# One front stage, loaded and ordered another way: scale columns first, shift columns last

## The reference, cut to what matters

```python
mod = (jax.nn.silu(c) @ p['w_ada'] + p['b_ada'])[:, None, :]
sh1, sc1, gt1, sh2, sc2, gt2 = jnp.split(mod, N_MOD, axis=-1)
hn = rms_norm(x, p['g_pre_mix']) * (1.0 + sc1) + sh1
proj = hn @ p['w_in']
```

## Time and profile before

| | |
|---|---|
| median of 3 runs | 1458.52 us (1458.16 to 1465.44) |
| profiled execution, its own time | 1462.23 us |
| its span | 1460.4 us |
| front stage, from the span's start to PE's last product in it | about 313 us |
| busy over the span | PE 87%, DVE 73%, ACT 52%, POOL 42% |

### The profile page before, as it was taken

One profiled execution on the slowest core, in us unless ns is written; L12 is line 12 of the kernel. 1 busy time (PEld: TensorE's weight loads), 2 busy tenths in 40 slices (PEclk: granted clock), 3 DMA queues, 4 the chain that ended last, 5 costly groups with the idle time before them and its releaser, 6 DMA issues. The chain is left out here.

```text
span 1460.4 us, 23246 instructions
## 1 busy us (share of the span) xinstructions
PE 1268.3 (87%) x6894; PEld 963.1 (66%) x6894; DVE 1069.1 (73%) x1980; ACT 753.6 (52%) x1609; POOL 616.1 (42%) x735
## 2 busy tenths in 40 slices
PE   5999999969898999699999998169999999999820
PEld 1688888855565656478888887048888888886300
DVE  3788878737786778557777764799999999993026
ACT  2432223213455758534444443148898899894134
POOL 1107767842232881012333221135665666564115
PEclk9999999987999989999999999579999999999975
DMA  9523444468987645324444453855989888879999
GB/s 328 154 83 127 160 159 173 151 217 315 310 283 208 183 159 162 129 100 144 144 144 146 166 163 131 310 189 144 279 250 273 242 221 260 247 184 301 374 294 356
DMA packets 111574, 305.35 MB, mean 209 GB/s; under 512 B 22884, under 2 KB 47589, under 8 KB 103758
## 3 DMA queue, kind: packets, MB, share of 16 engines
q1 hardware_dynamic: 85110, 230.90, 45.0%
q0 software_dynamic: 19360, 55.88, 16.3%
q10 hardware_dynamic: 7024, 17.60, 3.4%
HBM read 307.81 MB, written 97.21 MB: 277 GB/s over the span
## 5 line engine op out<-in xcount | busy, mean ns | idle before, releaser
L2943 DVE TENSOR_TENSOR ex_w_lo<-route_wgu,ex_w_hi 128x1024 fp32r<-128x1024 f32 x152 | 178.9, 1219 | 3.2 <-issue 2.4
L2671 POOL DMA_INDIRECT scratch_acc<-route_o,ex_to x43 | 83.6, 1944 | 186.6 <-DMA scratch_acc<-route_o,ex_to 108.5
L2712 ACT ACTIVATE ex_w_hi<-route_wgu 128x1024 fp32r (+1 forms) x152 | 152.8, 1065 | 6.0 <-issue 3.2
L147 PE MATMUL fr_ps_m<-fr_whi,fr_hl 128*128 128x512 f32 (+1 forms) x384 | 138.8, 362 | 1.0 <-DVE fr_wlo L657 0.5
L149 PE MATMUL fr_ps_m<-fr_whi,fr_hl 128*128 128x512 f32 (+1 forms) x384 | 136.1, 355 | 0.0
L148 PE MATMUL fr_ps_m<-fr_wlo,fr_hl 128*128 128x512 f32 (+1 forms) x384 | 136.0, 354 | 0.0
L2036 POOL TENSOR_SCALAR mx_st<-mx_st 128x1 f32<-128x1 f32 x68 | 38.7, 569 | 228.3 <-ACT mx_j L2084 128.1
L147 PE MATMUL ex_ps_h<-ex_w_hi,ex_xT 128*128 128x512 f32 x304 | 122.5, 403 | 0.2
L148 PE MATMUL ex_ps_h<-ex_w_lo,ex_xT 128*128 128x512 f32 x304 | 119.0, 391 | 0.0
L147 PE MATMUL mx_ps_m<-mw_area,mx_hT 128*128 128x512 f32 x272 | 108.9, 401 | 4.1 <-issue 2.1
L148 PE MATMUL mx_ps_m<-mw_area,mx_hT 128*128 128x512 f32 x272 | 107.3, 395 | 0.0
(11 more groups left out here) (549 smaller groups left out, 3482.1 us busy)
## 6 DMA issues: line engine op xcount, KB each, us to landing
route_wd<-in_w_exp_down_dram SPq DMA_DIRECT2D x47, 1024.0 KB, 12.9
route_wgu<-in_w_exp_gate_dram SPq DMA_DIRECT2D x46, 1024.0 KB, 10.8
route_wgu<-in_w_exp_up_dram SPq DMA_DIRECT2D x46, 1024.0 KB, 13.6
scratch_rec<-fr_w SPq DMA_DIRECT2D x16, 1048.0 KB, 4.1
s_rec<-scratch_rec SPq DMA_DIRECT2D x32, 524.0 KB, 5.9
scratch_proj<-fr_io SPq DMA_DIRECT2D x16, 640.0 KB, 3.0
scratch_acc<-in_zeros_dram SPq DMA_DIRECT2D x18, 512.0 KB, 5.6
fr_w<-in_w_ada_dram SPq DMA_DIRECT2D x8, 1024.0 KB, 9.1
```

Source lines behind the costliest of these rows:

```text
L147: nc.tensor.matmul(out, hi, w_hi, start=first, stop=False)
L2671: pool.indirect_dma_start(T["acc"], bass.IndirectOffsetOnAxis(to[:, t:t + 1], 0), o[:, t % 2, :], None, compute_op=ALU.add).then_inc(sem(" ...
L2712: A(w_hi[:, par, c * PW:(c + 1) * PW], wgu[:, bass.ds(slot * (KD * 2 * DE) + c * PW, PW)], ACT.Copy).then_inc(S["w_rounded"], 1)
L2943: vec.tensor_tensor(w_lo[:, par, c * PW:(c + 1) * PW], wgu[:, bass.ds(slot * (KD * 2 * DE) + c * PW, PW)], w_hi[:, par, c * PW:(c + 1) * P ...
```

## The change

The eight units of `w_ada` become eight scale units (512 KB each, loaded first) and eight shift units (512 KB each, loaded last, behind `w_in` and the parameters). `fold` becomes `fold_scale` and `fold_shift`. The transposes of the parameters move from between units 1 and 2 to behind the fourth product block of tile 0. `product(1)` moves ahead of the samples' products, which now stand between tiles 1 and 2; the shift units' matmuls, the shift rows and the samples' transposes stand inside tile 0's end and tile 1's product; the bias row is made in `product(2)` and not in `product(1)`. Tile 0's `add_bias` moves to t = 2 and stands behind `turns((4,))` and `turns((8,))`. New buffer `late` (3072 columns) holds two blocks of `w_in` first and then what `Bm`, `Bb`, `NB` and `kq` held; the samples' result goes to `samp` and no longer to `proj`, so `stored` counts one store less. The diff, cut to its core (SyncE, POOL, ACT, PE, DVE in this order):

```diff
+            def scale_unit(u):
+                sp.dma_start(scales[u], T["w_ada"][0, u * P:(u + 1) * P, D:2 * D]).then_inc(unit_in[u], 16)
+
+            def shift_unit(u):
+                if u >= 5:
+                    sp.wait_ge(mod_mm, KD + u - 2)
+                elif u >= 2:
+                    sp.wait_ge(mod_mm, KD)
+                sp.dma_start(shifts[u], T["w_ada"][0, u * P:(u + 1) * P, 0:D]).then_inc(unit_in[u], 16)
+
+            def rows_in(k):
+                if k >= 4:
+                    sp.wait_ge(mod_mm, 5)
+                sp.dma_start(raw[k], T["w_in"][0, k * P:(k + 1) * P, :]).then_inc(w_in[k], 16)
...
-            unit(0)
-            unit(1)
...
+            for u in range(6):
+                scale_unit(u)
+            sp.wait_ge(cT_done, 1)
+            sp.dma_start(x[:, 0, :], xp[:, 0, :]).then_inc(x_in[0], 16)
+            for u in range(6, KD):
+                scale_unit(u)
+            for k in range(4):
+                rows_in(k)
+            sp.dma_start(x[0:NS, 1, :], xs).then_inc(x_in[1], 16)
+            for k in range(4, KD):
+                rows_in(k)
...
-            for u in range(2, 4):
...
-            for k in range(KD):
...
+            for u in range(KD):
+                shift_unit(u)
             sp.wait_ge(s_out, SAMPLE_OUT)
-            sp.dma_start(pv[0:NS, NPT, :], proj[0:NS, 0, :]).then_inc(stored[0], 16)
+            sp.dma_start(pv[0:NS, NPT, :], samp[0:NS, :]).then_inc(small_out, 16)
...
-            pool.wait_ge(w_in[KD - 1], 16)
+            pool.wait_ge(s_mm, EARLY_MM)
...
-            pool.wait_ge(e_ready, 1)
+            pool.wait_ge(powers_ready, TURNS)
+            pool.wait_ge(s_out, BIAS_IN)
+            pool.wait_ge(small_out, 16)
...
                 act.wait_ge(rstd_ready, t + 2 if t else 1)
-                if t:
-                    act.wait_ge(stored[(t + 1) % 2], (t + 1) // 2 * 16)
+                if t >= 2:
+                    act.wait_ge(stored[(t + 1) % 2], t // 2 * 16)
...
             square(2)
+            root(2)
+            move(1)
             out(0)
-            move(1)
-            root(2)
+            turn_rates()
+            move_s()
+            out(1)
             square(3)
+            root(3)
+            move(2)
             out_s()
-            root(3)
-            for t in range(1, NPT):
+            square(4)
+            root(4)
+            for t in range(2, NPT):
                 if t + 1 < NPT:
                     move(t + 1)
-                if t == 1:
...
+                pe.wait_ge(unit_in[u], 16)
+                for a in range(2):
+                    last = nc.tensor.matmul(mod_bank[64 + 32 * a:96 + 32 * a, :], cT[:, u, :], scales[u][:, a * 512:(a + 1) * 512],
...
+                    elif t == 2 and c == 0:
                         pe.wait_ge(s_out, SAMPLE_OUT)
                         for b, (b0, n) in enumerate(cols):
-                            nc.tensor.matmul(ps_x[:, b, 0:n], ident[0:SR, NS:NS + 1].broadcast_to([SR, P]), proj[0:SR, 0, b0:b0 + n], start=True, stop=True).then_inc(s_mm, 1)
+                            nc.tensor.matmul(ps_x[:, b, 0:n], ident[0:SR, NS:NS + 1].broadcast_to([SR, P]), samp[0:SR, b0:b0 + n], start=True, stop=True).then_inc(s_mm, 1)
...
+                if k == 1 or k == KD - 1:
...
+            for u in range(6):
+                scale_unit(u)
             flip(0)
-            for u in range(5, 8):
-                unit(u)
-            pe.wait_ge(folded, 1)
+            for u in range(6, KD):
+                scale_unit(u)
+            pe.wait_ge(mod_done, 2)
             for j in range(4):
                 last = nc.tensor.transpose(mod_bank[:, j * P:(j + 1) * P], modB[:, j * P:(j + 1) * P], ident[:, :])
             last.then_inc(mods_mm, 1)
-            sample_rows()
+            gain_rows()
+            pe.wait_ge(moved_v, 2)
             for k in range(4):
                 first_product(k)
-            flip_s()
+            flip_params()
+            first_product(4)
+            first_product(5)
+            shift_unit(0)
+            shift_unit(1)
+            first_product(6)
+            flip(1)
+            first_product(7)
+            for u in range(2, 5):
+                shift_unit(u)
+            product(1)
+            for k in range(4):
...
+            flip(2)
             for k in range(4, KD):
-                first_product(k)
-                sample_product(k - 4)
-            sample_product(4)
-            flip(1)
-            for k in range(5, KD):
                 sample_product(k)
-            for t in range(1, NPT):
+            for t in range(2, NPT):
...
+            take_params()
+            mean(2)
+            invert(2)
+            move(1)
             angles()
-            mean(0)
-            mean(1)
-            invert(0)
...
+            fold_shift()
+            magnitudes()
             shift_s()
...
             powers()
+            mean(3)
+            invert(3)
             power_tables()
-            move(1)
-            invert(2)
-            mean(3)
+            move(2)
+            mean(4)
             inputs()
-            invert(3)
-            for t in range(1, NPT):
+            turns((0, 1, 2))
+            invert(4)
+            for t in range(2, NPT):
...
-                if t == 1:
-                    turns((0, 1, 2))
+                if t == 2:
+                    turns((4,))
+                    turns((8,))
+                    add_bias(0)
                 add_bias(t - 1)
                 if t + 2 < NPT:
                     mean(t + 3)
-                if t == 2:
-                    turns((4,))
-                    turns((8,))
                 for c in chunks_at(t - 1):
```

More of the change, by code:

```diff
@@ L221, in front @@
         modB, gain = t1, t2
-        NB, kq = s.sb("NB", [P, 2, 2, L, GC]), s.sb("kq", [GC, 2, 2, P])
+        NB = late[:, 0:512].rearrange("p (b g t c) -> p b g t c", b=2, g=2, t=L)
+        kq = late[0:GC, 512:1024].rearrange("p (b g n) -> p b g n", b=2, g=2)
         sgn = s.sb("sgn", [P, 1])
@@ L225, in front @@
         vi = s.sb("vi", [P, 2, NG], I32)
-        Bm, Cm, Bb = s.sb("Bm", [P, 2, NG, GC]), s.sb("Cm", [P, 2, NG, GC]), s.sb("Bb", [P, 2, NG, GC])
+        Bm, Bb = (late[:, a:a + 1024].rearrange("p (r g c) -> p r g c", r=2, g=NG) for a in (1024, 2048))
+        Cm = s.sb("Cm", [P, 2, NG, GC])
         pw = s.sb("pw", [P, 2, L + 1, NG])
@@ L439, in move_s @@
             def move_s():
-                act.wait_ge(t_done, 2)
+                act.wait_ge(t_done, 3)
                 load_x(2)
@@ L477, in split, with turn_rates @@
                 A(whi[:, k, :], raw[k], ACT.Copy, scale=gcol[:, k:k + 1]).then_inc(rounded, 1)
+            def turn_rates():
+                act.wait_ge(prepared, REDUCED)
+                A(V("sn", 3), V("red", 3), ACT.Sin).then_inc(sins, 1)
+                A(V("cs", 3), V("cred", 3), ACT.Sin).then_inc(sins, 1)
             square(0)
-            square(1)
-            act.wait_ge(reduced, 1)
-            A(V("sn", 3), V("red", 3), ACT.Sin).then_inc(sins, 1)
-            A(V("cs", 3), V("cred", 3), ACT.Sin).then_inc(sins, 1)
-            root(0)
-            root(1)
             move(0)
             act.wait_ge(prepared, GAINS)
-            for k in range(5):
-                split(k)
-            move_s()
+            split(0)
+            split(1)
+            root(0)
+            split(2)
+            split(3)
+            square(1)
+            split(4)
+            root(1)
             for k in range(5, KD):
@@ L755, in angles, with take_params @@
                 then(vec.tensor_copy(pick[:, :, NS:], by_row[:, :, 0:1].broadcast_to([P, 4, SR - NS])))
+            def take_params():
+                dve.wait_ge(mods_mm, PARAMS_FLIPPED)
+                st_.mark(vec.tensor_copy(V("lr"), ps_t[:, 0, 0:NG]))
+                st_.mark(vec.tensor_copy(V("li"), ps_t[:, 0, NG:2 * NG]))
+                st_.mark(vec.tensor_copy(d_c[:, :], ps_t[0:GC, 0, 64:64 + NG]))
+                for k in range(2):
+                    last = vec.tensor_copy(h0[:, k, :, :].rearrange("q b g -> q (b g)"), ps_t[:, 1, k * 2 * P:(k + 1) * 2 * P])
+                    if k == 0:
+                        st_.mark(last)
+                then(last)
                 dve.sem_inc(prepared, 1)
+                for r in range(2):
+                    st_.mark(vec.tensor_copy(Cm[:, r, :, :].rearrange("q g c -> q (g c)"), ps_x[:, 1 + r, :]))
+            def angles():
+                lr, li = V("lr"), V("li")
                 k2, f2, p2 = V("k", 3), V("f", 2), V("p", 2)
```

189 lines of the change are left out of this document (96 added, 93 removed).

## The result

| | before | changed |
|---|---|---|
| median of the runs, us | 1461.98 (1458.16 to 1469.15, 4 runs) | 1490.51 (1488.01 to 1491.95, 4 runs) |
| ratio, with its 95% interval | | 1.0206 (1.017 to 1.0241) |
| profiled execution: its time / its span | 1462.23 / 1460.4 | 1491.95 / 1489.8 |

The change makes the kernel 2.1% slower, 28.5 us by the medians and 29.4 us between the two profiled spans. The forecast was 26.3 more, 1485. Run once more, beside the experiments, the changed kernel stood at 1488.3 and 1.0188 (1.0162 to 1.0214) times the kernel before.

What follows compares the result with a forecast made beforehand. It took PE, full in the front stage's tile loop, as the bound; `product(3)` 24.4 us later (1.7 PE work, 22.7 waits) plus 1.9 clock loss gave +26.3, 1485 us, range 1474 to 1492.

Steps and rivals of the forecast that it cites:

- T: Time on PE when the last sample product ends and `flip(3)` starts, forecast at 90.6 us.
- clock lost behind `product(3)`: PE at half clock after the long wait before tile 3's product: 1.9 us lost, bounds 0 and 3.8.
- They land at about 36, PE waits 5.5 us: Parameters, queued behind the weights, land at about 36; PE waits 5.5 us at their transposes, after four product blocks.
- as they are issued ahead this time: Reason given for taking 4.5 us for the parameters' transfers, between 2.2 and 7.
- I take 2.5: The parameters' transposes on PE, taken at 2.5 us, ending at 38.5.
- the chain: From `flip(3)` through DVE's inputs, turns and `add_bias(0)`, the store and ACT's `out(2)` to `product(3)` at T+40.7.
- The sum above uses 1.07: Each half unit of `w_ada` on PE priced like a whole unit, 1.07 us; eight added passes cost 8.5.
- The other bound, 0.53: Lower bound for a half unit on PE, 0.53 us, which would make T 4.3 us earlier.
- A: Rival, slower by less: DVE reaches `inputs` without waiting for `square(4)`, 9 us earlier; +17, 1475.5 us; chance 0.09.
- B: Rival, no change: PE makes up the store wait over tiles 3 to 15; 1460 us; chance 0.05.
- C: Rival, faster: parameters by 33, cheap half units, full-clock transposes, no wait for DVE; 1452 us; chance 0.05.
- D: Rival, slower by more: parameters at 39 or later, T +3, clock falls twice, tables late once; +34, 1493; chance 0.06.

Runs made afterwards that it cites:

- tiny_first: Changed kernel with the seven small parameter transfers and rows 4 to 7 of `w_in` issued ahead of `c_re`, `c_im` and the states; 1483.57 us, ratio 1.0168.
- flip_late: Changed kernel with the parameters' transposes on TensorE moved behind the last block of the first product; 1478.93 us, ratio 1.0131.
- pair_shift: Changed kernel with odd and even shift units in different column groups, their halves added by the picking matrix; 1485.27 us, ratio 1.0159.
- square_early: Changed kernel with `square(4)` and `root(4)` on ScalarE moved ahead of `out_s`; 1480.8 us, ratio 1.0147.

## Why the prediction came out as it did

The direction and the mechanism were right: `add_bias(0)` behind all the turns on VectorE, the store of tile 0 behind it, and `out(2)`, for which `product(3)` waits. Term by term, on the profiled executions:

| term | forecast | measured |
|---|---|---|
| first product of tile 0 | 23.4 | 24.30 |
| parameters land | 36 | 41.8 |
| wait for them | 5.5 | 9.9 |
| end of their transposes | 38.5 | 45.0 |
| from there to `flip(3)`, T | 52.1, T = 90.6 | 52.2, T = 97.2 |
| `mean(4)` | T+2.8 | T+2.6 |
| turns start | T+11.6 | T+11.8 |
| `move(3)` done / wait at `flip(4)` | T+21.8 / 4.6 | T+21.9 / 5.1 |
| `add_bias(0)` | T+34.7 | T+34.9 |
| `product(3)` | T+40.7 | T+40.3 |
| clock lost behind `product(3)` | 1.9 | 1.4 |

**The step that failed is "They land at about 36, PE waits 5.5 us".** The parameters landed at 41.8 and PE waited 9.9. I priced them as bytes on the DMA queues, 4.5 us, and that was right for the large ones: DMA had moved them at 36.5. I put their issue at nothing, with the words "as they are issued ahead this time", and they were not. The change puts seven small transfers behind eight large ones on SyncE; behind the weights the eight held SyncE until 35.0, and the seven then needed 4.5 us more (35.01 to 39.48) with DMA nearly idle. tiny_first took 2.7 to 3.5 us of that wait away by order alone. flip_late left 1.4 of it, by putting other work into it.

**The transposes and the clock.** "I take 2.5" for them was 3.2, since all 9.9 us of idle time lie directly ahead: the granted clock fell to 0.50 in the wait and stayed there until about 48 us. The clock was charged once, behind the store; it was due here too. (The forecast reads the 3.15 us of the kernel before as the lower clock. The granted clock there is 1.00, but eight of the transposes took 1.97 us there; the same eight took 1.92 at 0.50 in the changed kernel and 1.04 at 1.00 in flip_late. So the duration fits the lower clock, and the clock column of that profile doesn't show it.)

**Luck in the 52.2.** From the transposes to `flip(3)` the forecast was 0.1 us off, because errors cancel. Product blocks 4 to 7 took 9.1 us and not 7.1, the first of them 3.3 (44.70 to 48.04) at the slow clock. Against that, the eight half units took 7.2 us and not 8.5, and the shift rows and the move of the samples 0.4 less each.

**The sum.** Measured in the profiles are T +6.3, the chain +24.3, the clock +1.4 (`product(3)` to the next tile's transposes took 15.24 us, before 13.86), and -2.6 for all that follows; the forecast had -0.3, +24.7 and +1.9. So the 26.3 missed 6.6 us at T, and was 3.5 too high elsewhere, of which 2.1 lie in the rest of the program, where the two profiles of the changed kernel alone differ by 3.9. The two have opposite signs, so that the total was only 3.1 off is partly luck too.

**Half units.** "The sum above uses 1.07": measured 1.05 for a half unit at the start and 0.92 to 0.96 for the shift units in a row. The other bound, 0.53, is out; pair_shift shows that the time of a half unit holds another half unit in the two column groups that it leaves empty.

**The rivals.** A ("DVE gets to `inputs` without waiting for `square(4)`") did not happen by itself; the run square_early makes it so by an edit, and gains 8.3 us where A has 9. In B the loop gives the wait back. It didn't: `product(3)` to the next stage was 0.9 us longer. C asked for `product(3)` within 18 us of `flip(3)`, and it came after 40.3. D ("parameters land at 39 or later and T with them") is what happened to T, at twice its +3, and the clock did fall twice; late tables, the rest of D, did not come. Its 1493 is nearer than my 1485, for two of its three reasons.
